# Row sums of the mixing weights on VectorE ahead of time; the second half's operand splits before the sample tile's gate; tiles aggregated one by one

## What is computed

```
p = h @ w_in;  uv = gelu(p[..., :2*E_B]);  z = p[..., 2*E_B:]      # E_B = 2048
u, v = split(uv);  v = layernorm(v, ln_g, ln_b)
ws = where(block_causal_mask, w_s, 0)                              # 8 groups of 128 x 128
mixed = einsum('gij,bcjgd->bcigd', ws, v5) + s_bias
s = (u * mixed) * silu(z);   out = s @ w_out
```

## Time and profile before

| | us |
|---|---|
| median of 3 runs | 2219.44 (2218.34 to 2219.84) |
| the profiled execution, its own time | 2218.88 |
| its span in the profile | 2217.1 |
| PE busy | 2205.6 (99%) |
| waits of PE, all that the list of waits has | 5.7 (2.2, 1.4 and 1.0 of them in the first 12 us) |
| DVE busy | 1596.1 (72%) |
| ACT busy | 968.1 (44%) |
| POOL busy | 358.1 (16%) |

### The profile page before, as it was taken

The page is one execution under the profiler, slowest core; times in us unless marked ns, Lnnn a source line. Parts: engine busy times, 40 slices in busy tenths (PEclk is TensorE's granted clock), DMA queues, the critical chain, the costliest instruction groups (busy, mean ns, idle before and its releaser), DMA issues.

```text
span 2217.1 us, 29967 instructions
## 1 busy us (share of the span) xinstructions
PE 2205.6 (99%) x11815; PEld 1942.0 (88%) x11815; DVE 1596.1 (72%) x1990; ACT 968.1 (44%) x1455; POOL 358.1 (16%) x517
## 2 busy tenths in 40 slices
PE   9999999999999999999999999999999999999998
PEld 7888899999888888888888888888889999998887
DVE  6789999997788988999986227852296666667321
ACT  7443333333453225665665125542236656666210
POOL 2111111111221112121110101210112121120000
PEclk9999999999999999999999999999999999999999
DMA  8555666564444313334346426352213333236321
GB/s 302 190 153 153 154 180 189 148 171 120 174 176 162 110 70 110 111 101 125 106 131 217 148 103 221 135 180 88 86 62 93 104 98 107 86 101 241 142 95 38
DMA packets 135436, 303.75 MB, mean 137 GB/s; under 512 B 18176, under 2 KB 54784, under 8 KB 133760
## 3 DMA queue, kind: packets, MB, share of 16 engines
q1 hardware_dynamic: 106192, 203.00, 27.6%
q0 software_dynamic: 28960, 98.57, 15.5%
q10 hardware_dynamic: 144, 0.26, 0.0%
HBM read 223.40 MB, written 78.75 MB: 136 GB/s over the span
## 4 chain that ended last, share of the span: by engine, by line
PE 98%; DMA 1%; DVE 0%; ACT 0%; SPq 0%; issue 0%; POOL 0%; DVEq 0%; POOLq 0%
PE PS L2357 31%; PE PS L2359 31%; PE PS L2358 31%; PE PS L2608 2%; PE PS L2364 1%; PE PS L2363 1%; PE PS L2450 1%; PE PS L2472 1%; DMA rawb<-wb_out_in 0%; DMA B22r<-wb_uz_in 0%; DMA raw<-wa_in_in 0%; PE PS L2459 0%; PE PS L2690 0%; PE PS L2613 0%; DVE S3l L1667 0%
## 5 line engine op out<-in xcount | busy, mean ns | idle before, releaser
L1729 DVE SCALAR_TENSOR_TENSOR acc<-cp,cw,acc 128x513 f32<-128x513 f32 (+3 forms) x464 | 366.9, 791 | 14.3
L2357 PE MATMUL PS<-HAh,Wh 128*128 128x512 f32 (+2 forms) x960 | 340.4, 355 | 3.7 <-DVE HAl L1672 2.2
L2358 PE MATMUL PS<-HAl,Wh 128*128 128x512 f32 (+2 forms) x960 | 338.7, 353 | 0.0
L2359 PE MATMUL PS<-HAh,Wl 128*128 128x512 f32 (+2 forms) x960 | 338.6, 353 | 0.0
L2357 PE MATMUL PS<-Vh,HBh 128*128 128x512 f32 x512 | 199.6, 390 | 0.0
L2359 PE MATMUL PS<-Vh,HBl 128*128 128x512 f32 x512 | 199.2, 389 | 0.0
L2358 PE MATMUL PS<-Vl,HBh 128*128 128x512 f32 x512 | 199.2, 389 | 0.0
L2357 PEld LDWEIGHTS PS<-HAh,Wh 128*128 128x128 f32 x960 | 180.4, 188 | 20.1 <-DVE Wl L1667 4.2
L2357 PE MATMUL PS<-Wbh,s7h 128*128 128x512 f32 x500 | 195.3, 391 | 0.0
L1756 DVE SCALAR_TENSOR_TENSOR over<-pair,cg,over 128x512 f32<-128x512 f32 (+1 forms) x240 | 189.9, 791 | 7.4
L2359 PE MATMUL PS<-Wbh,s7l 128*128 128x512 f32 x500 | 194.6, 389 | 0.0
(11 more groups left out here) (255 smaller groups left out, 5227.0 us busy)
## 6 DMA issues: line engine op xcount, KB each, us to landing
raw<-wa_in_in SPq DMA_DIRECT2D x48, 512.0 KB, 4.7
Wl<-wa_in_in POOLq DMA_DIRECT2D x39, 512.0 KB, 5.7
rawv<-wb_v_in SPq DMA_DIRECT2D x64, 256.0 KB, 5.0
QWr<-wb_uz_in SPq DMA_DIRECT2D x64, 256.0 KB, 2.6
v_scratch<-vb POOLq DMA_DIRECT2D x64, 256.0 KB, 2.6
vt<-v_scratch SPq DMA_DIRECT2D x32, 512.0 KB, 3.9
s_scratch<-m POOLq DMA_DIRECT2D x32, 512.0 KB, 4.0
rawb<-wb_out_in SPq DMA_DIRECT2D x28, 512.0 KB, 8.3
```

What stands on the lines that cost most here:

```text
L1729: return nc.vector.scalar_tensor_tensor(out=out, in0=src, scalar=w, in1=first, op0=ALU.mult, op1=ALU.add)
L2357: nc.tensor.matmul(out, wh, xh, start=start, stop=False, skip_group_check=seeded)
L2358: nc.tensor.matmul(out, wh, xl, start=False, stop=False, skip_group_check=seeded)
L2359: return nc.tensor.matmul(out, wl, xh, start=False, stop=stop, skip_group_check=seeded)
```

## The change

The row sums are no longer made by PE. The weights are loaded a second time with rows on the partitions (`wsi`, by SP in unit 8 of stage A); DVE reduces them in unit 12 with two instructions (the upper 64 rows over the first 64 columns, the lower 64 over all 128, so that no mask is needed); POOL stores the 128 x 8 result in unit 14 as 1024 single floats; SP loads it back in each half, broadcast to all partitions, into `rsb`. For half 0 SP issues three weight loads of block 1 (B12, B22, B11) ahead of the first `vt_load` instead of behind it. `bn_aggr` follows each tile's last `bn_stats`. In half 1 the splits of S3 and of S1's last piece, `copy_ab` and `copy_bc` stand ahead of the sample tile's gelu on ACT, and the low parts ahead of its sum and statistics on DVE. In half 0 only the writing of ACT's order differs, not the order.

```diff
@@ build @@
+    rs_d = nc.dram_tensor("row_sum_scratch", [1, GROUPS * P], fp32).ap()
+        wsum = g("wsum", [P, GROUPS])
+        wsi = at(m_at + 13312, "wsi", [P, GROUPS, P])
...
-            order = [("M1", 0), ("rs", 0)] + [(m, 0) for m in ("M6", "M2", "M7", "M5")]
+            order = [("M1", 0)] + [(m, 0) for m in ("M6", "M2", "M7", "M5")]
...
+        def v_at_end(h, q, i):
+            return (h, q, i) == (1, NQ - 1, len(TILES[1]) - 1)
@@ SP @@
+            def rows_load():
+                sp.dma_start(wsi[:, :, :], ws_i).then_inc(u_rows, 16)
+
+            def rsb_load(h):
+                if h == 0:
+                    sp.wait_ge(u_sums, 16)
+                else:
+                    sp.wait_ge(v_mm, V_DONE[h])
+                sp.dma_start(kp(rsb[:, :, :]), rs_d.to_broadcast([P, GROUPS * P])).then_inc(u_sbb, 16)
...
             def q_stage(h):
+                ahead = ("B12", "B22", "B11") if h == 0 else ()
+                for b in ahead:
+                    q_load(h, b, 1)
                 vt_load(h, 0)
                 if h == 0:
                     sp.wait_ge(q_slo, s_split(h, "S3"))
                     sbb_load(h)
+                rsb_load(h)
                 for j in range(KB):
                     if j + 1 < KB:
                         for b in ("B12", "B22", "B11", "B21"):
-                            q_load(h, b, j + 1)
+                            if j > 0 or b not in ahead:
+                                q_load(h, b, j + 1)
                         vt_load(h, j + 1)
...
+                if n == 8:
+                    rows_load()
@@ POOL @@
+                if n == 14:
+                    pool.wait_ge(u_rows, 18)
+                    nc.gpsimd.dma_start(rs_d.rearrange("o (g p) -> p (o g)", p=P), wsum[:, :],
+                                         allow_slow_non_contiguous=True).then_inc(u_sums, 16)
@@ ACT @@
+                        if v_at_end(h, q, i):
+                            s_high(h, "S3", slice(0, 1))
+                            copy_ab(h, 0)
+                            s_high(h, "S3", slice(1, 2))
+                            s_high(h, "S1", slice(1, 2))
                         if first + i == TAIL:
                             nc.scalar.activation(vb[u % 5][0:m, :], PS[low_half(TAIL), v_bank(h, q, i), :], ACT.Copy)\
                                 .then_inc(t_copy, 1)
+                            if v_at_end(h, q, i):
+                                copy_bc(h, 0)
                             act.wait_ge(t_sum, q + 2)
                         nc.scalar.activation(vb[u % 5][0:m, :], PS[0:m, v_bank(h, q, i), :], ACT.Gelu).then_inc(v_gel, 1)
...
-                if h == 1:
+                if h == 0:
+                    s_high(h, "S3")
                     copy_ab(h, 0)
-                s_high(h, "S3", slice(0, 1))
-                if h == 0:
-                    copy_ab(h, 0)
-                if h == 1:
-                    s_high(h, "S3", slice(1, 2))
-                    s_high(h, "S1", slice(1, 2))
-                copy_bc(h, 0)
-                if h == 0:
+                    copy_bc(h, 0)
@@ DVE @@
+                if (n, c) == (12, 0):
+                    row_sums()
...
+                        if v_at_end(h, q, i):
+                            s_low(h, "S3")
+                            s_low(h, "S1", slice(1, 2))
                         if t == TAIL:
                             tail_sum(PS[0:m, v_bank(h, q, i), :], vb[u % 5][0:m, :], q + 2)
                         dve.wait_ge(v_gel, u + 1)
                         nc.vector.bn_stats(vbs[0:m, i, q, :], vb[u % 5][0:m, :]).then_inc(v_bn, 1)
-                dve.wait_ge(v_bn, V_DONE[h])
-                dve.wait_ge(c_pad, 1)
-                for i, t in enumerate(TILES[h]):
-                    m = rows(t)
-                    nc.vector.bn_aggr(vmv[0:m, t, :], vbs[0:m, i, :, :]).then_inc(v_agg, 1)
+                        if q + 1 == NQ:
+                            if i == 0:
+                                dve.wait_ge(c_pad, 1)
+                            dve.wait_ge(v_bn, u + 1)
+                            nc.vector.bn_aggr(vmv[0:m, t, :], vbs[0:m, i, :, :]).then_inc(v_agg, 1)
...
-                nc.vector.tensor_copy(kp(rsb[:, :, :]), banks(MIX)).then_inc(u_rsb, 1)
+            def row_sums():
+                half = P // 2
+                dve.wait_ge(u_rows, 16)
+                nc.vector.tensor_reduce(wsum[0:half, :], wsi[0:half, :, 0:half], mybir.AxisListType.X, ALU.add)\
+                    .then_inc(u_rows, 1)
+                nc.vector.tensor_reduce(wsum[half:P, :], wsi[half:P, :, :], mybir.AxisListType.X, ALU.add).then_inc(u_rows, 1)
...
                 if j == 0:
-                    dve.wait_ge(u_sbb, 16 * (h + 1))
-                    dve.wait_ge(u_rsb, h + 1)
+                    dve.wait_ge(u_sbb, 32 * (h + 1))
@@ PE @@
-            def u_row_sums(h):
-                pe.wait_ge(u_mask, h + 1)
-                for i in range(2):
-                    pe.wait_ge(v_gel, v_last(h, MIX + i))
-                    last = nc.tensor.matmul(PS[:, MIX + i, :], one.to_broadcast([P, P]), kp(wst[:, 4 * i:4 * (i + 1), :]),
-                                            start=True, stop=True)
-                last.then_inc(u_rsmm, 1)
...
                 if j == 0:
-                    pe.wait_ge(u_rsb, h + 1)
-                    if h == 1:
-                        pe.wait_ge(v_gel, v_last(h, 5))
+                    pe.wait_ge(u_mask, h + 1)
+                    for b in range(5 if h == 1 else MIX, 8):
+                        pe.wait_ge(v_gel, v_last(h, b))
```

More of the change, by code:

```diff
@@ L98, in conv_plan, with build @@
     return steps, read, ends
-def build(nc, x, x_t0, x_t1, wa_in, wa_out, wb_v, wb_uz, wb_out, hist, conv_w, chan_par, pre_g, post_g, b_gb, ws_t, s_bias,
+def build(nc, x, x_t0, x_t1, wa_in, wa_out, wb_v, wb_uz, wb_out, hist, conv_w, chan_par, pre_g, post_g, b_gb, ws_t, ws_i, s_bias,
           consts, y_out, conv_out, v_out):
@@ L391, in build @@
             ("hi", "lo", "mm", "gel", "silu", "mu", "mz"))
-        u_ws, u_mask, u_rsmm, u_rsb, u_sbb = (sem(f"u_{n}") for n in ("ws", "mask", "rsmm", "rsb", "sbb"))
+        u_ws, u_mask, u_rows, u_sums, u_sbb = (sem(f"u_{n}") for n in ("ws", "mask", "rows", "sums", "sbb"))
         u_ldv, u_sub, u_vn, u_vo, u_add, u_mix, u_mev, u_sst, u_vst = (sem(f"u_{n}") for n in
@@ L1965, in v_norm @@
                 nc.vector.tensor_tensor(vo[:, :], vo[:, :], gb[:, 1, :], ALU.add).then_inc(u_vo, 1)
-            def u_sums(h):
-                dve.wait_ge(u_rsmm, h + 1)
-                if h == 0:
-                    dve.wait_ge(q_slo, s_split(h, "S3"))
-                nc.vector.tensor_copy(kp(rsb[:, :, :]), banks(MIX)).then_inc(u_rsb, 1)
+            def row_sums():
[4 more added lines that the diff above has]
+                nc.vector.tensor_reduce(wsum[half:P, :], wsi[half:P, :, :], mybir.AxisListType.X, ALU.add).then_inc(u_rows, 1)
             def u_add_bias(h, j):
                 if j == 0:
-                    dve.wait_ge(u_sbb, 16 * (h + 1))
-                    dve.wait_ge(u_rsb, h + 1)
+                    dve.wait_ge(u_sbb, 32 * (h + 1))
                 if h + j > 0:
@@ L2155, in q_stage @@
                 first, last = TILES[h][0], SUBS[h] - 1
-                s_low(h, "S3")
                 if h == 0:
+                    s_low(h, "S3")
                     s_add(h, "S4a")
@@ L2162, in q_stage @@
                                                    op0=ALU.mult, op1=ALU.mult).then_inc(v_neg, 1)
-                if h == 1:
-                    s_low(h, "S1", slice(1, 2))
-                u_sums(h)
                 if h == 0:
@@ L2656, in q_stage @@
                         u_mixing(h, i)
-                    elif m == "rs":
-                        u_row_sums(h)
                     else:
@@ L2839 @@
         "ws_t": np.asarray(b_w_s)[0].transpose(2, 0, 1),
+        "ws_i": np.asarray(b_w_s)[0].transpose(1, 0, 2),
         "s_bias": np.asarray(b_s_bias)[0].reshape(1, GROUPS * P),
```

## The result

| | median us | against before |
|---|---|---|
| before (6 runs) | 2219.11 (2218.34 to 2219.84) | |
| changed (6 runs) | 2229.78 (2229.65 to 2232.43) | 1.0050 (1.0037 to 1.0063) |

The change costs 10.7 us, 0.5%. The forecast was 2220.6 with a range up to 2224.0: the time is outside it. Nearest is rival (e), the small pieces, which had 2225.6 and a chance of 0.13; its sign was a wait of over 2 us at unit 17, and that is there.

A forecast was written before the change was run, and what follows sets the result against it. PE, busy 99% of the span, was taken as the bound. Stage A +1.2, half 0 -1.4 and half 1 +1.4 gave +1.2 us on 2218.88: 2220.1, or 2220.6 as a median, range 2217.6 to 2224.0.

The forecast's parts named there:

- rival (e): Stage A: the 1024 small pieces hold the queue ahead of unit 17's `Wl`; 2225.6 with the full 5 us, chance 0.13.
- The small store: Stage A, unit 14: POOL's 4 KB store delays unit 17's `Wl` by between 0 and 5 us; taken as 0.
- The reductions: Stage A: 1.75 us more on DVE against 0.6 us of cover; PE waits 1.15 us at unit 17, plus 0.1 restart.
- the delay is hidden as far as DVE's own results go: Stage A: PE waited for none of DVE's chunks after the first 12 us, so DVE's 1.75 us delay would not reach PE directly.
- Half 0: M6 0.8 us earlier, the 0.5 us wait before step 1's M1 gone, restart 0.1: -1.4 us, range -1.6 to -0.8.
- the 0.5 us for `QW`: Half 0: loads issued ahead remove PE's wait for the low part of `QW` before step 1's M1, 0.5 us gained.
- Half 1: 1.35 us gained at first, then overtaken by the late gelu and v: +1.4 us, range +0.6 to +2.1.
- The first gains: Half 1: M6 gains about 1.0 us of 1.72 and M7 loses its 0.34 us wait: 1.35 us.
- their return before sub 1's M1 and M3: Half 1: these wait for ACT work behind the late gelu; PE keeps only about 0.55 of 1.35 us.
- `v_norm` waiting for the gain rows: Half 1: gain rows issued 3.9 us later, so `v_norm` starts at 1664.5 to 1666.0 instead of 1662.57.
- The victim: Half 1: late `v_norm` delays DVE's low part, so block 1's M1 starts at 1673.15 to 1674.7 instead of 1672.59.
- Stage V: Aggregating tile by tile costs DVE some 0.25 us a tile in half 1, not needed before 1652, and nothing in half 0.

The follow-up runs named there:

- e6: Kernel before plus only the store of 1024 single floats in unit 14 (constant tile, read by nothing): 2227.15 us, +8.9 over before.
- e3: Changed kernel with the row sums' store written as 128 pieces of 32 bytes instead of 1024 of 4: 2222.60 us, +4.3 over before.
- e4: Changed kernel with the same store issued from SP's hardware queue in unit 15, not POOL's software queue: 2228.45 us, +10.2 over before.
- e1: Changed kernel with only POOL's store of the row sums moved from unit 14 to unit 38: 2222.26 us, +4.0 over before.
- e5: Kernel before plus only the second weight load (unit 8) and the two reductions (unit 12), result unused: 2222.11 us, +3.9 over before.
- e2: Changed kernel with the store moved to unit 38 and the two reductions to unit 18: 2222.93 us, +4.7 over before.
- e14: Kernel before, unchanged, run and profiled a second time: 2218.15 us against 2218.71 for the same kernel.
- e10: Changed kernel with second weight load, reductions and store moved from stage A to stage V of half 0: 2220.73 us, +2.5 over before.
- e11: e10 with half 1's order as before, sample tile's gelu and statistics first: 2219.10 us, +0.9 over before.
- e13: e10 with only S3's first three quarters and `copy_ab` between the sample tile's gate steps in half 1: 2216.81 us, -1.9 against before.
- e12: e10 with half 0's three weight loads of block 1 back behind the load of v: 2222.67 us, +4.0 over before.

## Why the prediction was wrong

- **The small store, taken as 0 with a bound of 5.** This is the step that failed. I bounded it by the gate's stores, which "have as many pieces"; but theirs are 512 bytes long, not 4. The bound from above was too low: `Wl` took 6.3 us longer to land (7.2 in e6), and the store itself 9.9 to 12.8 us after its issue in the kernels that had it. How the 4 KB are cut is what counts (e3), not the queue (e4). The Trainium skill (DMA: Bandwidth & Descriptors, Specifications) says that a piece below 512 B is done as read, modify, write; the prediction quoted it and kept 0. e3 shows that being below 512 B isn't enough to be slow: 128 pieces of 32 B landed in 3.8 us.
- **The clock after a long wait, not in the sum.** +2.0 us, shown by the windows. Rival (e) named the store and its sign, and its 2225.6 was still 4.2 us short: 2.0 for the clock, 1.3 for the bound's overrun, 0.6 in half 1. Its mechanism, the place in the queue, isn't needed (e4).
- **The reductions, +1.15 at unit 17.** Their duration was nearly right, 1.95 us for 1.75. At unit 17 they cost 0.5 to 0.6 us where they stand without the store (e1, e3, e5), because `Wl` landed in 5.5 and 5.6 us there and not in 6.6. The step that "the delay is hidden as far as DVE's own results go" was wrong: e1, e2 and e5 show a wait of 1.6 to 2.5 us at the end of A, some 360 us later. I had taken "PE waited for none of its chunks in the whole of A" as slack; at the end of A there was none. In the changed kernel itself this cost nothing, because the other wait covered it; in e1 it is the largest loss in the trace.
- **Half 0, -1.4.** Right in size against the profile of before, -1.4 in Q: M6's wait for `copy_ab` 0.76 us (0.6 to 0.8 forecast), no wait for `QW`. But the 0.5 us for `QW` was read from one execution, and e5, e6 and e14 haven't that wait: against them the loads ahead gain nothing, and half 0 is worth 0.7. The agreement is luck to that extent.
- **Half 1, +1.4, range +0.6 to +2.1.** +2.0 measured. The first gains (M6, M7: -1.2 for -1.35), their return before sub 1's M1 and M3 (1.0 us for 0.8), and `v_norm` waiting for the gain rows came as described, and `v_norm` started at 1665.4 in before's time (1674.43 less the 9.0 us by which PE was late when half 1 began), within 1664.5 to 1666.0. The victim was mis-named: I followed the chain to DVE's low part and block 1's M1, and passed by that `copy_bc` for sub 1's M5 stands on ACT behind the high part of the same weights. That M5 is due 1.6 us before M1 (1671.01 against 1672.59 before).
- **Stage V.** That `bn_aggr` tile by tile costs nothing held: no wait of PE before Q in half 0.

Shown by runs: the store, the way it is cut, that POOL's queue isn't needed, the reductions' cost at the end of A, the gate's order, the loads' worth beside a load of `rsb`. Only read from traces: the slow clock's 2.0 us at unit 17 (no run had so long a wait without it; the 2.08 us of e3 and e4 are the nearest pair), and the masking of DVE's loss by PE's wait, which the sums of e5 and e6 support. Open: why the convolution's store lands later in e1, e3, e5, e10, e11 and e13 than in the two profiles of before, and what spreads single executions of one kernel by 1 to 5 us (e12: 2221.59 to 2226.83). Part of that spread goes with the clock: e12's three executions over 2225 have mean granted clocks of 0.997 and 0.998, its other eight 0.999 or 1.000. What the 4-byte pieces hold, the DMA engines or the memory behind them, was not tried.

## What to carry to other kernels

A store's price is in its pieces, not its bytes: 4 KB as 1024 floats took longer to land than 512 KB of weights, and the bill goes to the DMAs issued behind it, on its own queue or the other one in use (e4); put it where no landing is awaited for 20 us (SP's load behind the store landed at 210 us, the store was issued at 190), or make the pieces longer. An engine without rest carries each added microsecond to the next place where the bound engine has no slack against it, however far: look at every consumer along the chain, not the next one only. A wait read from one execution is not yet a gain: take a second profile of the kernel before, and see if it is still there. And when an order is changed on one engine, list all that stands behind the late instruction, in order; the first of them that the bound engine needs is the one that waits.

## What the runs showed of the hardware

- A wait of PE of 7.6 us was followed by nine products at a granted clock of 0.50, the 1.2 GHz level, at 0.43 us each where 0.23 is the pitch at 2.4 GHz. The same after 6.0 and 6.6 us (e4 and e6, 12 and 13 products), after the 2.10 us of e5 at the end of A, and after the 2.50 us in e2, whose 364-column products then had a pitch of 0.30 us; after the 1.6 us of e1 and the 1.9 us of e3 at the same place the windows keep 1.00. Two waits of 2.08 us at one place in half 1 went either way: 1.00 in e3, 0.55 in e4.
- 1024 pieces of 4 bytes to DRAM: POOL's issue 0.90 us, landing 9.9 to 12.6 us from POOL, 12.8 us from SP (issue 0.43 us). 128 pieces of 32 bytes: issue 0.56 us, landing 3.8 us. A 512 KB load issued 3 us behind the former in POOL's queue landed in 12.9 and 13.8 us, one issued 5 us behind it with the store in SP's queue in 11.4 us, instead of 5.5 to 6.6. In the changed kernel the DMA share was 0 from 194 to 197 us. SP's load of 512 KB, issued 8 to 11 us behind the store: 9.0 to 11.5 us instead of 3.5 to 4.8.
- A float32 reduction of 64 x 512 took 0.67 us and one of 64 x 1024 took 1.22 us, as additions of those lengths do. The Trainium skill (VectorE: DVE Perf Modes, the perf-mode tier table) puts a reduction in the 1x mode; these rows agree.
